# Gate logits as one stacked product, sample states in one burst, and small columns behind four tiles of x

## The chip, the cores and the metric

The kernel runs on one core of one Trainium2 chip. The core has a matrix engine (TensorE, PE in the profile, with PEld for its weight loads), a vector engine (VectorE, DVE), a scalar engine (ScalarE, ACT), GpSimd (POOL) and a queue engine (SyncE, SP), and 16 DMA engines. The metric is the device time of one execution in microseconds; a kernel is told by the median of its runs.

## What is computed

One step of a decoder with two post-norm layers over 1024 prompt tokens and 64 sample tokens (8 sequences of 8). Its first part is one projection x @ w_in, whose columns feed a gated linear attention (GLA), a forgetting attention, a short convolution and merge gates. The change touches only the GLA part:

```python
a_pre = jnp.einsum('btr,rk->btk', p['gla_a'], w_gla_a2) + b_gla_a          # r = 16
log_a = (jax.nn.log_sigmoid(a_pre.astype(jnp.float32)) / GLA_TAU).reshape(B, T, GLA_H, GLA_DK)
...
b = jnp.cumsum(log_a.astype(f32).reshape(B, N, C, H, DK), axis=2)
b_last = b[:, :, -1:]
...
k_end = kf * jnp.exp(b_last - b)
ds = jnp.einsum('bnthk,bnshv->bnhkv', k_end, vf)
def step(S, inp):
    d, dS = inp
    return d[..., None] * S + dS, S
```

The 16 columns `gla_a` times `w_gla_a2` are the gate logits. For the sample sequences one step gives the new state of each of 8 batches and 4 heads: the old state decayed, plus ds.

## The kernel before, in words

The work stands in four stages; the change lies in the first, `stage_front`. Every engine has its own program, written out in order, and engines wait for each other on semaphores that only count up. Nothing is scheduled automatically: an engine's order is the order of the code in its block.

**Projection.** x is loaded in 9 tiles of up to 128 tokens (`load_x` on SP), transposed by TensorE (`transpose_x`, 8 transposes a tile into a ring of 6 banks) and split into a high part `xh` (ScalarE, `x_heads`) and a low part `xl` (VectorE, `x_tails`). Weights come in blocks of 128 columns (`load_block`, two raw buffers) and are split likewise: ScalarE's `head(n)` writes `w_hi`, VectorE's `tail(n)` writes `w_lo` and so frees the raw buffer, for which the load of block n + 2 waits. A product is three matmuls, high by high, high by low, low by high, over 8 chunks of 128 rows.

**Units.** `FRONT` lists the order of the column blocks, and each entry makes units: three groups of tokens (384, 384, 320), or nine for v. `work` computes a unit into bank n % 2 and so waits until the unit two before it has been read out, which the reader tells by counting up `unit_free`. `place` reads a unit out, on ScalarE or VectorE by kind. The first entry, s, is a block of small columns: 8 of the forget logits and 16 of `gla_a` (at column 32), with zeros between. Its three units s0, s1, s2 stand among the transposes: s0 behind three tiles that have been split, s1 and s2 behind all nine. Then come the a units (gate logits, one FP32 matmul of `wa2` by `gaT` each), then the v units.

On ScalarE the head of block 1 and 2 stands behind the read-out of s0, that of block 3 behind s1's, and `place` of s copies `gaT` (line 594) and then the forget logits `z` (line 595), which gives the bank back.

On VectorE `place` of an s unit does nothing before the change. Its place in the order, for all three, is behind the splits of blocks 1, 2 and 3:

```python
            x_tails(0, 6)
            tail(0)
            x_tails(6, 18)
            tail(1)
            tail(2)
            tail(3)
            for n in range(first("s", 0), first("v", 0)):
                place(n)
```

**Recurrence.** For each pair of heads p, TensorE alternates `attend`, `new_state` and `outputs` per tile with `fill`, which computes quarters of projection units. After the last tile come the sample states: `new_sample_state` for two batches at a time, into banks 5 and 6, each of the later ones waiting for VectorE's `carry_sample` of the two before (`s0_new`), with a `fill` between. Scores are in banks 3 and 4. Then, for p = 0, the second a units.

## Time and profile before

| what | us |
|---|---|
| median of 3 runs | 1643.15 |
| the runs | 1642.85 to 1646.71 |
| the profiled execution | 1645.76 |
| its span, from first to last instruction | 1644.1 |
| TensorE busy in it | 1529.4 (93%) |
| VectorE busy | 829.7 (50%) |
| ScalarE busy | 663.8 (40%) |
| GpSimd busy | 236.1 (14%) |

The mean granted TensorE clock was 0.972 of 2.4 GHz. Times in the rows below count from the span's start. A busy time of TensorE includes matmuls that overlap, so the distance from one matmul's start to the next tells its price better than its length. Idle time of an engine off the critical path costs nothing.

### The profile page before, as it was taken

Reading aid. Unit: us, or ns where it says so; the run is one execution under the profiler, and the core shown is the slowest. Engines: PE = TensorE matmul, PEld = TensorE weight load, DVE = VectorE, ACT = ScalarE, POOL = GpSimd, SP = SyncE. Lnnn points to the kernel's source line nnn. Section 1 sums busy time; section 2 is a strip of 40 time slices with the busy share of each in tenths; the row PEclk is TensorE's granted clock in tenths of the full one; section 3 lists DMA queues with packets and bytes.
Section 4 is the critical chain, followed back from the end, with each engine's and each line's share of the span. In section 5 each row is a group of like instructions: output and inputs, shape, how many; then the busy total and the mean of one; then the engine's idle time right before and its main releaser. Section 6 shows DMA issues by size and latency. Waiting matters only on the chain. (4 is left out here: it accounts for less than half of the span.)

```text
span 1644.1 us, 26139 instructions
## 1 busy us (share of the span) xinstructions
PE 1529.4 (93%) x10051; PEld 1394.5 (85%) x10051; DVE 829.7 (50%) x1386; ACT 663.8 (40%) x1135; POOL 236.1 (14%) x295
## 2 busy tenths in 40 slices
PE   8999999999999998999999999999995799999980
PEld 7999899899987887889999999998784688888760
DVE  4422463353045654522332232223758699999975
ACT  5422242222255554422121121113111688888866
POOL 1000120013012111130000000000000334543310
PEclk9999999999999999999999999999996899999995
DMA  6121232134212121173261124103535799999646
GB/s 189 36 45 39 81 119 54 29 92 147 81 50 72 44 72 59 36 244 125 62 205 39 39 59 150 56 1 117 179 116 167 241 269 276 340 297 283 164 64 237
DMA packets 154229, 204.39 MB, mean 124 GB/s; under 512 B 14723, under 2 KB 121235, under 8 KB 154104
## 3 DMA queue, kind: packets, MB, share of 16 engines
q1 hardware_dynamic: 135224, 140.82, 27.4%
q0 software_dynamic: 18880, 61.89, 13.8%
q8 instruction: 80, 1.31, 0.3%
q14 instruction: 45, 0.37, 0.1%
HBM read 152.34 MB, written 50.34 MB: 123 GB/s over the span
## 5 line engine op out<-in xcount | busy, mean ns | idle before, releaser
L388 PE MATMUL ps<-xh,slab_hi 128*128 128x384 f32 (+1 forms) x504 | 170.4, 338 | 1.3 <-DVE slab_lo L752 1.3
L388 PE MATMUL ps<-xh,slab_lo 128*128 128x384 f32 (+1 forms) x504 | 165.0, 327 | 0.0
L388 PE MATMUL ps<-xl,slab_hi 128*128 128x384 f32 (+1 forms) x504 | 164.8, 327 | 0.0
L1921 PE MATMUL ps<-xh,slab_lo 128*128 128x384 f32 (+1 forms) x384 | 125.2, 326 | 0.0
L1921 PE MATMUL ps<-xh,slab_hi 128*128 128x384 f32 (+1 forms) x384 | 125.1, 326 | 0.0
L1921 PE MATMUL ps<-xl,slab_hi 128*128 128x384 f32 (+1 forms) x384 | 125.1, 326 | 0.0
L2137 DVE TENSOR_TENSOR gt_sg<-ps,gt_sg 128x384 f32<-128x384 f32 (+1 forms) x48 | 25.7, 536 | 187.6 <-PE ps L1921 187.5
L2913 PE MATMUL ps<-mo_hi_gu,mo_xh 128*128 128x512 f32 x256 | 100.3, 397 | 1.2 <-ACT mo_xh L3016 0.7
L388 PEld LDWEIGHTS ps<-xh,slab_hi 128*128 128x128 f32 x504 | 95.1, 189 | 6.7 <-issue 5.4
L2077 ACT ACTIVATE gt_sg<-ps 128x384 f32<-128x384 f32 (+1 forms) x48 | 22.7, 473 | 192.2 <-PE ps L1921 192.2
L2913 PE MATMUL ps<-mo_hi_gu,mo_xl 128*128 128x512 f32 x256 | 99.4, 393 | 0.0
L388 PEld LDWEIGHTS ps<-xl,slab_hi 128*128 128x128 f32 x504 | 95.1, 189 | 0.0
L388 PEld LDWEIGHTS ps<-xh,slab_lo 128*128 128x128 f32 x504 | 95.0, 189 | 0.0
L1921 PE MATMUL ps<-gt_oh,slab_hi 128*128 128x384 f32 (+1 forms) x288 | 94.0, 327 | 0.0
L1921 PE MATMUL ps<-gt_oh,slab_lo 128*128 128x384 f32 (+1 forms) x288 | 94.0, 326 | 0.0
L1921 PE MATMUL ps<-gt_ol,slab_hi 128*128 128x384 f32 (+1 forms) x288 | 94.0, 326 | 0.0
L2867 POOL DMA_INDIRECT acc_dram<-mo_y,mo_slot_idx x32 | 71.8, 2243 | 141.6 <-DMA acc_dram<-mo_y,mo_slot_idx 73.7
L3089 DVE TENSOR_TENSOR mo_lo_gu<-mo_raw_g,mo_hi_gu 128x2048 fp32r<-128x2048 f32 x32 | 73.3, 2290 | 15.4 <-issue 12.2
L2871 POOL MEMSET mo_small<- 128x1 f32 x1 | 0.1, 98 | 522.3 <-POOLq L74 522.3
L1218 PE MATMUL ps<-xh,slab_hi 128*128 128x384 f32 (+1 forms) x192 | 69.8, 363 | 5.7 <-ACT slab_raw L1340 3.9
L2920 PE MATMUL ps<-mo_lo_gu,mo_xh 128*128 128x512 f32 x256 | 67.2, 404 | 7.0 <-DVE mo_lo_gu L3089 6.9
L3089 DVE TENSOR_TENSOR mo_lo_gu<-mo_raw_u,mo_hi_gu 128x2048 fp32r<-128x2048 f32 x32 | 73.1, 2283 | 0.4 <-issue 0.3
(500 smaller groups left out, 4053.1 us busy)
## 6 DMA issues: line engine op xcount, KB each, us to landing
slab_raw<-in_w_in SPq DMA_DIRECT2D x60, 512.0 KB, 4.4
mo_raw_g<-in_w_e_gate SPq DMA_DIRECT2D x16, 1024.0 KB, 11.1
mo_raw_u<-in_w_e_up SPq DMA_DIRECT2D x16, 1024.0 KB, 14.6
mo_raw_d<-in_w_e_down SPq DMA_DIRECT2D x16, 1024.0 KB
gt_oh<-oT_hi SPq DMA_DIRECT2D x3, 2176.0 KB, 8.9
gt_ol<-oT_lo SPq DMA_DIRECT2D x3, 2176.0 KB, 13.8
slab_raw<-in_w_branch SPq DMA_DIRECT2D x24, 256.0 KB, 4.5
x_dram<-slab_raw SPq DMA_DIRECT2D x9, 512.0 KB, 5.2
```

The lines of the kernel that those rows point to most:

```text
L388: mm = eng.matmul(out, w[:, b, k, :], x[:, k, t0:t0 + tn], start=(k == 0 and j == 0), stop=(k == KC - 1 and j == 2), skip_group_check=True)
L1218: mm = eng.matmul(out, w[:, b % RH, k, :], x[:, k, t0:t0 + tn], start=(k == 0 and j == 0), stop=(k == KC - 1 and j == 2), skip_group_check ...
L1921: last = eng.matmul(out, w[:, s % 2, c, wk, :], x[:, k, t0:t0 + tn], start=(k == 0 and i == 0), stop=(k == ks[-1] and i == 2))
L2077: eng.activation(sg[:, v % 4, 0:tn], sh.ps[:, gate_bank(j, v), 0:tn], ACT.Sigmoid).then_inc(sg_ready, 1)
L2137: eng.tensor_tensor(sg[:, v % 4, 0:tn], sh.ps[:, branch_bank(v), 0:tn], sg[:, v % 4, 0:tn], ALU.mult).then_inc(mul_done, 1)
L2867: eng.indirect_dma_start(out=sh.acc_dram[:, :], out_offset=bass.IndirectOffsetOnAxis(ap=mo.slot_idx[:, i:i + 1], axis=0), in_=y[:, i % RY, ...
L2871: eng.memset(small[:, :], EPS / ALPHA ** 2).then_inc(small_set, 1)
L2913: eng.matmul(sh.ps[:, 2 + r, :], (xh, xl)[j][:, r, k, :], hi_gu[:, r, k].rearrange("p m n -> p (m n)"), start=(k == 0 and j == 0), stop=False)
L2920: last = eng.matmul(sh.ps[:, 2 + r, :], xh[:, r, k, :], lo_gu[:, r, k].rearrange("p m n -> p (m n)"), start=False, stop=(k == KC - 1))
L3089: eng.tensor_tensor(lo_gu[:, i % 2, :, m, :], from_raw(buf, side, KC), f32(hi_gu[:, i % 2, :, m, :]), ALU.subtract).then_inc(tail_gu, 1)
```

## The change

Three things are changed, all in `stage_front`.

The small columns: SP loads x tiles 0 to 3, not only 0 and 1, before the two loads of small columns. GpSimd then copies the 16 columns of `gla_a` to columns 64 and 96 of the raw block as well, so that s has three copies of them, and ScalarE's `head(0)` waits for those copies.

The gate logits: `wa2` is loaded three times, at rows 32, 64 and 96 of a cleared tile, and split into `wa2S` with high rows at 32 and 96 and low rows at 64. `gaS` holds the read-out of an s unit, 112 rows, high at 32 and 64 and low at 96. One matmul in F32R format then sums all three partial products. The low rows are subtracted on VectorE, in `place`, and it is VectorE's subtraction that now gives the unit's bank back. The a units wait until all three s units have been given back.

The sample states: `new_sample_states` computes those of all 8 batches at once, into banks 3 and 4, ahead of the four fills; it waits for the scores to be read. `carry_sample` on VectorE keeps its places.

```diff
+    GA_AT, GA_ROWS = (32, 64, 96), 112
...
-        gaT, wa2 = sb("gaT", [LR, TOK]), sb("wa2", [LR, 256])
+        gaS = sb("gaS", [GA_ROWS, TOK], F32R)
+        wa2, wa2S = sb("wa2", [GA_ROWS, 256]), sb("wa2S", [GA_ROWS, 256], F32R)
...
+        def new_bank(b):
+            return sh.ps[:, 3 + b // 4, 128 * (b % 4):128 * (b % 4) + DV]
...
+            eng.memset(wa2[:, :], 0.0)
             eng.memset(w_raw[:, 0], 0.0).then_inc(cleared, 1)
...
+            eng.wait_ge(w_in[0], 32)
+            for at in GA_AT[1:]:
+                last = eng.tensor_copy(w_raw[:, 0, :, at:at + LR], w_raw[:, 0, :, GA_AT[0]:GA_AT[0] + LR])
+            last.then_inc(cleared, 1)
...
-            load_x(0)
-            load_x(1)
+            for t in range(4):
+                load_x(t)
             eng.wait_ge(cleared, 1)
             for col, at, n in ((FF, 0, H_FOX), (GA, 32, LR)):
                 eng.dma_start(w_raw[:, 0, :, at:at + n], sh.w_in[0, :, col:col + n].rearrange("(k p) n -> p k n", p=128)
                               ).then_inc(w_in[0], 16)
-            for t in range(2, NT):
+            for t in range(4, NT):
                 load_x(t)
...
-            eng.dma_start(wa2[:, :], sh.w_gla_a2[0]).then_inc(c_in, 16)
+            for at in GA_AT:
+                eng.dma_start(wa2[at:at + LR, :], sh.w_gla_a2[0]).then_inc(c_in, 16)
...
                     if kind == "a":
-                        eng.wait_ge(s_out, 3)
+                        for m in range(3):
+                            freed(eng, "s", 0, m)
...
                 if kind == "a":
                     t0, tn = GROUPS[g]
-                    mm = eng.matmul(out, wa2[:, 128 * i:128 * i + 128], gaT[:, t0:t0 + tn], start=True, stop=True)
+                    mm = eng.matmul(out, wa2S[:, 128 * i:128 * i + 128], gaS[:, t0:t0 + tn], start=True, stop=True)
...
-                eng.wait_ge(c_in, 96)
+                eng.wait_ge(c_in, 128)
...
+                if i == NT:
+                    eng.wait_ge(s0_new, 4)
...
-            def new_sample_state(p, b2):
-                if b2 == 0:
-                    eng.wait_ge(kes_ready, p + 1)
-                    eng.wait_ge(s_ready, s_count(p, NCH))
-                else:
-                    eng.wait_ge(s0_new, 4 * p + b2)
-                for e in range(2):
+            def new_sample_states(p):
+                eng.wait_ge(kes_ready, p + 1)
+                eng.wait_ge(att_ready, NT * (p + 1))
+                for b in range(DB):
                     for h in range(2):
-                        mm = eng.matmul(sh.ps[half(h), 5 + e, 0:DV], kez_s[:, 2 * b2 + e, half(h)],
-                                        v[0:64, p, NT - 1, 128 * h:128 * h + 128], start=True, stop=True,
-                                        skip_group_check=True)
+                        mm = eng.matmul(new_bank(b)[half(h), :], kez_s[:, b, half(h)], v[0:64, p, NT - 1, 128 * h:128 * h + 128],
+                                        start=True, stop=True, skip_group_check=True)
                 mm.then_inc(dss_mm, 1)
...
+                new_sample_states(p)
                 for b2 in range(4):
-                    new_sample_state(p, b2)
                     fill(p, 3 * NT + b2)
...
-                eng.wait_ge(w_in[n % RW], 16 * (n // RW + 1) + (16 if n % RW == 0 else 0))
+                if n == 0:
+                    eng.wait_ge(cleared, 2)
+                else:
+                    eng.wait_ge(w_in[n % RW], 16 * (n // RW + 1) + (16 if n % RW == 0 else 0))
                 eng.activation(w_hi[:, place_of(n)], w_raw[:, n % RW], ACT.Copy).then_inc(w_head, 1)
...
                 if kind == "s":
                     if g == 0:
-                        eng.wait_ge(c_in, 96)
-                    eng.activation(gaT[:, t0:t0 + tn], bank[32:48, :], ACT.Copy).then_inc(s_out, 1)
-                    eng.activation(z[:, t0:t0 + tn], bank[0:8, :], ACT.Identity, bias=bf[:, :]).then_inc(free, 1)
+                        eng.wait_ge(c_in, 128)
+                        eng.activation(wa2S[:, :], wa2[:, :], ACT.Copy)
+                    eng.activation(z[:, t0:t0 + tn], bank[0:8, :], ACT.Identity, bias=bf[:, :])
+                    eng.activation(gaS[:, t0:t0 + tn], bank[0:GA_ROWS, :], ACT.Copy).then_inc(s_out, 1)
...
+                if kind == "s":
+                    eng.wait_ge(s_out, g + 1)
+                    if g == 0:
+                        low = slice(GA_AT[1], GA_AT[1] + LR)
+                        eng.tensor_tensor(wa2S[low, :], wa2[low, :], f32(wa2S[low, :]), ALU.subtract)
+                    low = slice(GA_AT[2], GA_AT[2] + LR)
+                    eng.tensor_tensor(gaS[low, t0:t0 + tn], bank[low, :], f32(gaS[low, t0:t0 + tn]), ALU.subtract).then_inc(free, 1)
...
-                        eng.wait_ge(dss_mm, 4)
+                        eng.wait_ge(dss_mm, 1)
...
-                eng.wait_ge(dss_mm, 4 * p + b2 + 1)
+                eng.wait_ge(dss_mm, p + 1)
...
-                    last = eng.scalar_tensor_tensor(out=S0[:, b, :], in0=S0[:, b, :], scalar=d, in1=sh.ps[:, 5 + e, 0:DV],
+                    last = eng.scalar_tensor_tensor(out=S0[:, b, :], in0=S0[:, b, :], scalar=d, in1=new_bank(b),
                                                     op0=ALU.mult, op1=ALU.add)
```

The program's order on VectorE at the start. `w_lo` is in `slab_lo`; the four rows of line 752 are `tail` of blocks 1 to 4. Before:

```order
L760 TENSOR_TENSOR xl<-ps,xh 128x4x128 [waits fr_x_head] x6
L752 TENSOR_TENSOR slab_lo<-slab_raw,slab_hi 128x1024 [waits fr_w_head]
L760 TENSOR_TENSOR xl<-ps,xh 128x4x128 [waits fr_x_head] x10
L760 TENSOR_TENSOR xl<-ps,xh 128x4x64 [waits fr_x_head] x2
L752 TENSOR_TENSOR slab_lo<-slab_raw,slab_hi 128x1024 [waits fr_w_head] x4
L976 COPY fr_cols<-ps 128x76 [waits fr_b2_mm]
```

After:

```order
L766 TENSOR_TENSOR slab_lo<-slab_raw,slab_hi 128x1024 [waits fr_w_head] x3
L787 TENSOR_TENSOR fr_wa2S<-fr_wa,fr_wa2S 16x256 [waits fr_s_out]
L789 TENSOR_TENSOR fr_gaS<-ps,fr_gaS 16x384
L789 TENSOR_TENSOR fr_gaS<-ps,fr_gaS 16x384 [waits fr_s_out]
L789 TENSOR_TENSOR fr_gaS<-ps,fr_gaS 16x320 [waits fr_s_out]
L766 TENSOR_TENSOR slab_lo<-slab_raw,slab_hi 128x1024 [waits fr_w_head]
L997 COPY fr_cols<-ps 128x76 [waits fr_b2_mm]
```

Four subtractions have come in, the one that gives back the bank of s0 behind the splits of blocks 1 to 3 and ahead of that of block 4.

ScalarE from the last x split to the first copy of an a unit (`fr_T`). Line 574, after it 587, is `head`: blocks 1 and 2, then 3, then 4. Before:

```order
L594 ACTIVATE fr_gaT<-ps 16x384 [waits fr_c_in,fr_unit_mm]
L595 ACTIVATE fr_wide<-ps,fr_bf 8x384
L574 ACTIVATE slab_hi<-slab_raw 128x1024 [waits fr_w_in1]
L574 ACTIVATE slab_hi<-slab_raw 128x1024 [waits fr_w_in0]
L594 ACTIVATE fr_gaT<-ps 16x384 [waits fr_unit_mm]
L595 ACTIVATE fr_wide<-ps,fr_bf 8x384
L574 ACTIVATE slab_hi<-slab_raw 128x1024 [waits fr_w_in1]
L594 ACTIVATE fr_gaT<-ps 16x320 [waits fr_unit_mm]
L595 ACTIVATE fr_wide<-ps,fr_bf 8x320
L574 ACTIVATE slab_hi<-slab_raw 128x1024 [waits fr_w_in0,fr_unit_mm]
L602 ACTIVATE fr_T<-ps,fr_bga 128x384 [waits fr_pool_s,fr_unit_mm]
```

After:

```order
L607 ACTIVATE fr_wa2S<-fr_wa 112x256 [waits fr_c_in,fr_unit_mm]
L608 ACTIVATE fr_wide<-ps,fr_bf 8x384
L609 ACTIVATE fr_gaS<-ps 112x384
L587 ACTIVATE slab_hi<-slab_raw 128x1024 [waits fr_w_in1]
L587 ACTIVATE slab_hi<-slab_raw 128x1024 [waits fr_w_in0]
L608 ACTIVATE fr_wide<-ps,fr_bf 8x384 [waits fr_unit_mm]
L609 ACTIVATE fr_gaS<-ps 112x384
L587 ACTIVATE slab_hi<-slab_raw 128x1024 [waits fr_w_in1]
L608 ACTIVATE fr_wide<-ps,fr_bf 8x320 [waits fr_unit_mm]
L609 ACTIVATE fr_gaS<-ps 112x320
L587 ACTIVATE slab_hi<-slab_raw 128x1024 [waits fr_w_in0,fr_unit_mm]
L616 ACTIVATE fr_T<-ps,fr_bga 128x384 [waits fr_pool_s,fr_unit_mm]
```

A copy of `wa2S` has come in, and the logits (`fr_wide`) now come ahead of the `gaS` copy that stands in for `gaT`.

On TensorE, at the end of the first pair of heads, the last sample matmuls of `outputs` (line 497, after it 511), the sample states (509, after it 520) and the first product of a unit behind them. Before:

```order
L497 MATMUL ps<-fr_T,fr_qz 64x128 [waits fr_o_mm,fr_state_in]
L497 MATMUL ps<-fr_T,fr_qz 64x128 x15
...
L509 MATMUL ps<-fr_wide 64x128 [waits fr_s_ready,fr_kes_ready]
L509 MATMUL ps<-fr_wide 64x128 x3
...
L388 MATMUL ps<-xh,slab_hi 128x384 [waits fr_w_tail,fr_unit_free0]
...
L509 MATMUL ps<-fr_wide 64x128 [waits fr_s0_new]
L509 MATMUL ps<-fr_wide 64x128 x3
```

After:

```order
L511 MATMUL ps<-fr_T,fr_qz 64x128 [waits fr_o_mm,fr_state_in]
L511 MATMUL ps<-fr_T,fr_qz 64x128 x15
...
L520 MATMUL ps<-fr_wide 64x128 [waits fr_att_ready,fr_kes_ready]
L520 MATMUL ps<-fr_wide 64x128 x15
...
L400 MATMUL ps<-xh,slab_hi 128x384 [waits fr_w_tail,fr_unit_free0]
```

The four groups of four matmuls (the second of them is shown as well; two more follow in the same way) have become one group of sixteen ahead of the fills. The profile counts two passes for each of these FP32 matmuls.

## Rows read from the trace of the kernel before

**Rows 1.** The page, the span in 40 equal slices: busy tenths of TensorE.

```profile
PE   8999999999999998999999999999995799999980
```

**Rows 2.** Busy time by stage: stretch, its length, PE, PEld, DVE, ACT, POOL, PEclk, DMA, GB/s.

```profile
0.00:40.00 40.00, 31.91 (x167) 28.39 (x168) 17.07 (x24) 21.11 (x34) 7.21 (x26) 0.92 0.68 194
...
800.00:1000.00 200.00, 200.00 (x1217) 200.00 (x1216) 59.32 (x78) 33.35 (x37) 0.00 (x0) 1.00 0.34 103
```

**Rows 3.** Timeline of TensorE in the front: start, length, instruction [idle before, releaser].

```profile
9.04 3.67 PE L408 MATMUL ps<-ident,fr_wide 128*128 128x128 f32 x16 [0.72 <-DMA fr_wide<-in_x_prompt]
13.99 0.66 PE L388 MATMUL ps<-xh,slab_hi 128*128 128x384 f32 x1 [1.28 <-DVE slab_lo L752]
...
19.57 4.30 PE L408 MATMUL ps<-ident,fr_wide 128*128 128x128 f32 x40
...
28.09 0.31 PE L388 MATMUL ps<-xh,slab_hi 128*128 128x320 f32 x1
...
31.46 0.31 PE L388 MATMUL ps<-xh,slab_lo 128*128 128x320 f32 x1
...
33.53 3.70 PE L377 MATMUL ps<-fr_gaT,fr_wa 16*128 16x384 f32 x6 [1.41 <-ACT fr_gaT L594]
37.15 0.58 PE L382 MATMUL ps<-slab_hi,xh 128*128 128x256 f32 x1
```

**Rows 4.** Timeline of ScalarE in the front.

```profile
11.54 1.05 ACT L574 ACTIVATE slab_hi<-slab_raw 128x1024 fp32r<-128x1024 f32 x1
...
31.87 1.06 ACT L574 ACTIVATE slab_hi<-slab_raw 128x1024 fp32r<-128x1024 f32 x1 [2.50 <-DMA slab_raw<-in_w_in]
32.95 0.43 ACT L594 ACTIVATE fr_gaT<-ps 16x320 f32<-16x320 f32 x1
33.41 0.52 ACT L595 ACTIVATE fr_wide<-ps,fr_bf 8x320 f32<-8x320 f32 x1
```

**Rows 5.** By stage as above, two half microseconds of the front: the last column is GB/s.

```profile
6.00:6.50 0.50, 0.50 (x4) 0.50 (x3) 0.07 (x1) 0.40 (x1) 0.50 (x1) 1.00 0.90 89
...
7.50:8.00 0.50, 0.50 (x4) 0.42 (x2) 0.47 (x1) 0.49 (x1) 0.42 (x2) 1.00 0.97 385
```

**Rows 6.** Timeline of GpSimd (first row) and of VectorE in the front.

```profile
3.55 0.29 POOL L270 CAST fr_mask<-fr_T 128x128 int32<-128x128 f32 x1
...
10.82 0.69 DVE L760 TENSOR_TENSOR xl<-ps,xh 128x512 fp32r<-128x512 f32 x1 [1.14 <-ACT xh L581]
...
26.87 2.36 DVE L752 TENSOR_TENSOR slab_lo<-slab_raw,slab_hi 128x1024 fp32r<-128x1024 f32 x2 [0.50 <-ACT slab_hi L574]
32.96 1.23 DVE L752 TENSOR_TENSOR slab_lo<-slab_raw,slab_hi 128x1024 fp32r<-128x1024 f32 x1 [3.73 <-ACT slab_hi L574]
```

**Rows 7.** By stage: the first v products, with the granted clock.

```profile
37.10:40.50 3.40, 3.40 (x16) 3.35 (x16) 0.00 (x0) 1.64 (x2) 0.00 (x0) 0.50 0.62 169
```

**Rows 8.** Timeline of TensorE around the first group of new sample states.

```profile
175.53 1.96 PE L497 MATMUL ps<-fr_T,fr_qz 64*64 64x128 f32 x32
177.42 0.41 PE L388 MATMUL ps<-xh,slab_hi 128*128 128x320 f32 x1
...
180.02 0.31 PE L388 MATMUL ps<-xh,slab_lo 128*128 128x320 f32 x1
180.26 0.65 PE L509 MATMUL ps<-fr_wide 64*64 64x128 f32 x8
180.84 0.41 PE L388 MATMUL ps<-xh,slab_hi 128*128 128x320 f32 x1
...
181.09 0.30 PE L388 MATMUL ps<-xl,slab_hi 128*128 128x320 f32 x1
```

**Rows 9.** Timeline at the second a units: TensorE, and ScalarE's copies of them.

```profile
196.16 1.56 PE L377 MATMUL ps<-fr_gaT,fr_wa 16*128 16x384 f32 x4
198.72 0.80 PE L377 MATMUL ps<-fr_gaT,fr_wa 16*128 16x320 f32 x2 [1.01 <-ACT fr_T L602]
...
198.11 1.03 ACT L602 ACTIVATE fr_T<-ps,fr_bga 128x384 f32<-128x384 f32 x2
```

More of the change, by code:

```diff
@@ L768, in place @@
                     eng.wait_ge(unit_mm, n + 1)
-                if kind == "k":
+                if kind == "s":
[5 more added lines that the diff above has]
+                    eng.tensor_tensor(gaS[low, t0:t0 + tn], bank[low, :], f32(gaS[low, t0:t0 + tn]), ALU.subtract).then_inc(free, 1)
+                elif kind == "k":
                     eng.wait_ge(e12, 2 * i + 2)
```

## The prediction

> **What bounds the kernel now.** I read the slices first: TensorE shows 8 or 9 tenths in nearly every slice up to about 1230 us [rows 1], and a long stage such as 800 to 1000 us is 200.00 us busy out of 200.00, while the first 40 us hold 31.91 us [rows 2]. The reader is to see that the front, which the change touches, lies at the head of one long queue of TensorE: whatever delays or advances TensorE there moves all that follows, unless a later wait hangs on something that did not move. So I price the change at two points of TensorE's timeline: the first v product at 37.15 us [rows 3] and the length of the pieces that are altered near 180 us, 196 us and 340 us.
>
> Then I followed TensorE through the front row by row [rows 3]: the transposes of the third x tile at 9.04 after a wait of 0.72 for its data, unit s0 from 13.99 after a wait for `w_lo` of the small columns, transposes again at 19.57, then s1, and s2 straight behind it at 28.09, ending at 31.46 + 0.31 = 31.77. The a products start at 33.53, after a wait of 1.41 for ScalarE's copy of `gaT`. That copy (32.95) stands in ScalarE's queue behind the split of weight block 3 (31.87), which waited 2.50 for its transfer [rows 4].
>
> **Small columns behind four tiles.** SP now issues x tiles 0 to 3 first. Gain: the third tile no longer waits behind the columns, so at most the 0.72 us goes, and the head of block 0 moves from 11.54 to 10.8 at best [rows 3, 4]. Price: the columns land later. In the trace the rate sinks to 89 GB/s while they move, and is back at 385 GB/s by 7.5 us, so they had landed by then [rows 5]. Two more tiles of 524 KB at 385 GB/s ahead of them cost 2.7 us: 10.2. GpSimd's two new copies of 128 x 128 elements are bounded by the 0.29 us of a cast of that size [rows 6]; they make 10.8. GpSimd has finished its clears by then or just after. So the columns arrive when the tiles do; I take -0.7 for s0, with bounds -0.72 and +1.8 (columns landing 2.5 us later than worked out). Two more small loads on SP and a clear of `wa2` on GpSimd lie ahead of nothing that is late: block 3, the transfer that is waited for, is issued only when block 1 has been split.
>
> **Stacked product: the wait it adds.** Unit s0's bank is now given back not by ScalarE but by VectorE, in `place("s", 0)`. In VectorE's queue that stands behind the splits of blocks 1, 2 and 3, as the order in the section on the change shows. Unit s2 writes the same bank, so s2 now waits for the split of block 3. Queued behind s2 on TensorE is everything else. Step by step: VectorE's split of block 1 ends at 26.87 + 1.18 = 28.05 (half of the 2.36 for two) [rows 6]; it comes 0.7 earlier by the step above, and 0.35 later for ScalarE's new copy of `wa2S` (256 columns; the 320-column copy takes 0.43 [rows 4]): 27.7. Head 3 started 31.87 - 28.05 = 3.8 later, its transfer in between: 31.5. The split on VectorE starts 1.09 behind it and takes 1.23 [rows 4, 6]: 32.6 to 33.8. Then VectorE's two new subtractions of 256 and 384 columns; a 512-column one took 0.69 [rows 6], so I take 0.35 + 0.52, between nothing and 1.4 for both: s2 starts at **34.7** where it started at 28.09. TensorE stands idle for some 7 us.
>
> How long s2 then takes is not in the trace, since it ran at the full level: 3.68. After the shorter idle at 32 us the granted clock was 0.50, the lower level of 1.2 GHz, with 16 v products of 256 columns in 3.40 us, or 0.2125 each [rows 7]. At that rate 24 products of 320 columns take 6.4 us. The nearest row is s0: 24 products of 384 columns took 5.58 (13.99 to 19.57), and at the rate of s2's 320 columns, 0.147 apiece, they would have taken 4.2; it began slow and recovered, at a price of 1.4 [rows 3]. I take the same 1.4: 5.1, bounds 3.68 and 6.4. s2 ends at **39.8**.
>
> **Stacked product: from s2 to v.** ScalarE's bias copy (0.52), then its stacked copy (0.43) [rows 4], then VectorE's subtraction of 320 columns (about 0.45): the first a product at 41.3. ScalarE puts the head of block 4 (1.06 as for block 3) behind its copy, so its first copy of an a product starts 2.0 after s2; at 0.51 each [rows 9] two of them end 3.1 after s2. The third a product waits for the first, the first v product for the second: 39.8 + 3.15 = **42.95**, against 37.15. The front loses **5.8 us**; with s2's bounds +4.4 to +7.1, and to +8.9 if the columns are late as well. The products themselves are cheaper: from 33.53 to 37.15 the old three took 3.62, the new three 1.65, and that is inside the sum. I leave the v products as slow at their beginning as before, since a stretch of the same kind stands ahead of them.
>
> The Trainium skill ("FP8 and Floating Point Precision", section TensorE Precision Notes) says that a true FP32 product makes four passes through the array. By that alone the three products would shrink to a quarter, 0.9 instead of 1.65 in the front, and likewise near 196 us; how far the trace bears that out is weighed among the rivals.
>
> At the second a unit (196.16) the first two products take 1.56 and the third waits 1.01 for ScalarE's copy at 198.11 [rows 9]. That copy waits for a splitting chain, not for the products, so it stays; of the gain only the third product is left, 0.80 against the 0.31 of a 320-column product: **-0.4**, bounds 0 and -1.0.
>
> **New sample states in one burst.** Before, four groups of eight passes; each interrupts the unit in progress. From the product at 180.02 to the one behind the group at 180.84 there are 0.82 us, and the next follows after 0.25 instead of 0.147: 0.82 - 0.147 + 0.10 = 0.78 a group, 3.1 for four. In a burst: the 32 passes at 175.53 took 1.89 up to 177.42 [rows 8]; with the turn into and out of the burst, 2.15. That gives -0.95 per pair of heads, **-1.9** for both, bounds -1.4 and -2.4. The waits on `s0_new` that go price nothing extra: a group that waits for it comes out of the same 0.78 that the first, which doesn't, costs. The new wait on `att_ready` has already been met by `outputs`, and `attend` of the second pair waits for updates that ended tens of microseconds ahead. VectorE's eight updates keep their places and have more slack.
>
> **Sum.** +5.8 - 1.9 - 0.4 = +3.5 us. Against the profiled execution's 1645.76 that is 1649.3; its span is 1644.1. The median of the three runs is 1643.15, 2.6 lower, and it is the median that I carry: **1646.7**.
>
> **Rivals.** (a) *The lower clock lasts longer.* Place: s2 and the first v products. If s2 runs wholly at 1.2 GHz it takes 6.4 (+1.3), and if the v products stay there another 3.4 us, as in the stretch of [rows 7], half of that is lost (+1.7): +6.5, 1649.7, slower. It decides from 1.4 us of extra loss on. For it: 7 us of idle where 1.4 sufficed for a fall. Against it: s0 recovered midway. 0.22.
> (b) *No second fall.* s2 brings the clock up and the short waits before v don't bring it down: the 1.7 that the v products lose now comes back: +1.8, 1645.0. Against it: just such waits led to the 0.50. 0.15.
> (c) *Columns late.* If they land 2.5 us after the estimate, s0 and all behind it go from -0.7 to +1.8: +6.0, 1649.2. For it: the rate of 89 GB/s. 0.08.
> (d) *The bank is free in time,* so that the change costs no wait: s0's gain, the burst and the a unit alone: -0.7 - 1.9 - 0.4 = -3.0, 1640.2. Against it: the order on VectorE. 0.05.
> (e) *The a products bound by the array,* not by ScalarE's copies: their 1088 columns at the 0.2125 per 256 of [rows 7] are 0.9 in place of the 1.65 from the first of them to v (-0.75), and in the second unit the third product's wait of 1.01 goes too: +3.5 - 0.75 - 1.0 = +1.75, 1644.9. Against it: the third product waited for ScalarE [rows 9]. 0.05. By the Trainium skill ("FP8 and Floating Point Precision", TensorE Precision Notes) this is how the time would come out; the row at 198.72 does not agree.
> The forecast itself, 0.42, and 0.03 for a gain beyond these.
>
> **How the numbers follow.** A measurement of this kernel can tell about 0.3%, 4.9 us, from no change. Faster than 1638.2 needs a gain that I have no row for: 0.03. Slower than 1648.1: (a), (c) and 0.05 of the forecast's own upper end: 0.35. The rest, 0.62, is within it. The range, 1642.3 to 1651.0, leaves out (d), the gain without a row and what (a) and (c) could add to each other; it takes in (b) and (e) with some of the burst's bounds below them, since the runs before alone lie up to 3.9 us apart.
>
> **What would show it.** Of the changed kernel: TensorE's first 320-column product of s2 near 34.7 with some 7 us of idle released by VectorE's subtraction into `gaS`; the first v product near 43; head 0 near 10.8; each burst near 2.1 us with no group inside the fills; the third a product near 196 us still waiting for ScalarE. I am wrong if s2 follows s1 at once, if the front's delay does not reach the end, or if the clock's levels in the front cost more than 1.5 us other than worked out.

## The result, and the profile after

The changed kernel is **slower by 0.3%**: 1649.8 us (median of 9 runs, 1646.88 to 1653.72) against 1644.4 (9 runs, 1642.85 to 1648.42) on the same chip, ratio 1.003 with an interval of 1.0021 to 1.0039. The forecast was 1646.7, within a range of 1642.3 to 1651.0. The profiled execution after took 1649.8 us with a span of 1648.2, 4.1 longer than before, at a mean granted clock of 0.966 (before 0.972). Of the runs further down, one of e10 (3856.59 us) and one of the kernel before (3717.15 us) took more than twice as long and are in no ratio.

TensorE in the front after, as [rows 3] show it before. Columns: start, length, instruction, [idle before, releaser].

```profile
4.72 5.08 PE L420 MATMUL ps<-ident,fr_wide 128*128 128x128 f32 x32 [4.72 <-DMA fr_wide<-in_x_prompt]
12.75 0.41 PE L400 MATMUL ps<-xh,slab_hi 128*128 128x384 f32 x1 [2.95 <-DVE slab_lo L766]
...
16.99 4.29 PE L420 MATMUL ps<-ident,fr_wide 128*128 128x128 f32 x40
...
32.81 0.61 PE L400 MATMUL ps<-xh,slab_hi 128*128 128x320 f32 x1 [7.17 <-DVE fr_gaS L789]
...
38.91 0.42 PE L429 MATMUL ps<-ident,fr_T 19*128 19x19 f32 x4
40.53 0.64 PE L389 MATMUL ps<-fr_gaS,fr_wa2S 112*128 112x384 f32 x2 [1.20 <-DVE fr_gaS L789]
41.62 0.64 PE L389 MATMUL ps<-fr_gaS,fr_wa2S 112*128 112x320 f32 x1 [0.44 <-ACT fr_T L616]
42.09 0.58 PE L394 MATMUL ps<-slab_hi,xh 128*128 128x256 f32 x1
```

The gap of 0.72 ahead of the third x tile is gone, s0 starts 1.24 earlier, and then TensorE stands still for 7.17 us ahead of s2 and waits for VectorE's write of `gaS`. The first v product comes at 42.09 instead of 37.15: **4.94 us lost in the front**.

VectorE behind that wait (compare [rows 6]):

```profile
24.21 2.36 DVE L766 TENSOR_TENSOR slab_lo<-slab_raw,slab_hi 128x1024 fp32r<-128x1024 f32 x2 [0.41 <-ACT slab_hi L587]
30.42 1.23 DVE L766 TENSOR_TENSOR slab_lo<-slab_raw,slab_hi 128x1024 fp32r<-128x1024 f32 x1 [3.85 <-ACT slab_hi L587]
31.67 0.42 DVE L787 TENSOR_TENSOR fr_wa2S<-fr_wa,fr_wa2S 16x256 fp32r<-16x256 f32 x1
32.10 1.04 DVE L789 TENSOR_TENSOR fr_gaS<-ps,fr_gaS 16x384 fp32r<-16x384 f32 x2
39.89 0.50 DVE L789 TENSOR_TENSOR fr_gaS<-ps,fr_gaS 16x320 fp32r<-16x320 f32 x1 [6.74 <-ACT fr_gaS L609]
```

and ScalarE, whose head of block 3 sets the second row above (compare [rows 4]):

```profile
10.29 1.06 ACT L587 ACTIVATE slab_hi<-slab_raw 128x1024 fp32r<-128x1024 f32 x1 [0.67 <-POOL slab_raw L290]
...
29.33 1.06 ACT L587 ACTIVATE slab_hi<-slab_raw 128x1024 fp32r<-128x1024 f32 x1 [2.70 <-DMA slab_raw<-in_w_in]
...
39.02 0.52 ACT L608 ACTIVATE fr_wide<-ps,fr_bf 8x320 f32<-8x320 f32 x1 [8.64 <-PE ps L400]
39.45 0.41 ACT L609 ACTIVATE fr_gaS<-ps 112x320 fp32r<-112x320 f32 x1
...
40.98 1.05 ACT L616 ACTIVATE fr_T<-ps,fr_bga 128x384 f32<-128x384 f32 x2 [0.18 <-PE ps L389]
```

The chain is read backwards: s2 waits for the subtraction at 32.10, that stands behind the split at 30.42, that waits for ScalarE's head at 29.33, and that for the transfer of block 3 (2.70).

Head 0, at 10.29, is released by GpSimd, whose copies of the columns stand straight behind its clears:

```profile
9.14 0.53 POOL L287 MEMSET slab_raw<- 128x512 f32 x1
9.73 0.53 POOL L290 COPY slab_raw<-slab_raw 128x128 f32<-128x128 f32 x2
```

So the columns had landed by 9.73, and it was GpSimd's queue, not a load, that head 0 and with it s0 waited for.

Stretches of the front and two later ones (compare [rows 2, 7]). Columns: stretch, its length, PE, PEld, DVE, ACT and POOL busy with instruction counts, granted clock, DMA share, GB/s.

```profile
0.00:40.00 40.00, 24.50 (x148) 23.38 (x148) 16.99 (x26) 17.05 (x31) 8.03 (x29) 0.87 0.64 182
12.75:16.95 4.20, 4.20 (x24) 4.20 (x25) 1.05 (x2) 0.00 (x0) 0.00 (x0) 1.00 1.11 302
27.90:32.80 4.90, 0.00 (x0) 0.02 (x1) 2.34 (x4) 1.06 (x1) 0.00 (x0) 0.50 0.58 154
32.80:38.90 6.10, 6.09 (x24) 5.92 (x24) 0.34 (x1) 0.00 (x0) 0.00 (x0) 0.56 0.30 84
...
42.10:45.00 2.90, 2.90 (x14) 2.90 (x14) 0.23 (x1) 1.64 (x2) 0.00 (x0) 0.50 0.61 168
202.00:205.40 3.40, 3.16 (x10) 3.02 (x11) 1.15 (x2) 3.13 (x11) 2.06 (x4) 0.50 0.63 151
800.00:1000.00 200.00, 200.00 (x1218) 200.00 (x1217) 60.93 (x81) 32.86 (x36) 0.00 (x0) 1.00 0.32 96
```

Three things are to be seen. s0 ran at the full 2.4 GHz from its first product: clock 1.00, and 24 products in 4.24 us. (So early the clock column alone does not tell it: in the trace of before it reads 1.00 from 13.99 to 16.80 too, where the products stand 0.32 us apart, twice the 0.17 of s0 after the change.) The clock was already at the lower level of 1.2 GHz while TensorE stood idle, so s2 ran at it almost to its end (0.56): 6.10 us. And the long stage from 800 to 1000 us is as dense as before, so it gives nothing back.

The burst and the second a units (compare [rows 8, 9]), both from TensorE's timeline:

```profile
184.63 0.31 PE L400 MATMUL ps<-xh,slab_lo 128*128 128x320 f32 x1
184.87 1.96 PE L520 MATMUL ps<-fr_wide 64*64 64x128 f32 x32
186.77 0.41 PE L400 MATMUL ps<-xh,slab_hi 128*128 128x320 f32 x1
...
199.58 0.33 PE L389 MATMUL ps<-fr_gaS,fr_wa2S 112*128 112x384 f32 x1
200.32 0.44 PE L389 MATMUL ps<-fr_gaS,fr_wa2S 112*128 112x384 f32 x1 [0.41 <-DVE fr_y L839]
202.24 0.64 PE L389 MATMUL ps<-fr_gaS,fr_wa2S 112*128 112x320 f32 x1 [1.47 <-ACT fr_T L616]
...
202.74 0.67 PE L400 MATMUL ps<-xh,slab_hi 128*128 128x384 f32 x1
```

From the product ahead of the burst to the one behind it there are 2.14 us. The third a product still waits for ScalarE, 1.47 where it was 1.01, and the clock falls at 202.0, just there; that it falls because of this wait is not shown (see e6 and e9 below).

Where the difference stands along TensorE's timeline (start of the same instruction, after minus before):

| at (us, before) | place | after - before |
|---|---|---|
| 37.15 | first v product | +4.94 |
| 175.53 | ahead of the first burst | +4.61 |
| 196.16 | second a units | +3.42 |
| 199.45 | behind them | +3.21 |
| 211.41 | transposes of the outputs | +4.51 |
| 332.27 | ahead of the second burst | +3.94 |
| 347.23 | behind it | +2.85 |
| 636.33 | end of the first layer's attention | +4.40 |
| 742.79 | behind the transposes of cached keys | +5.59 |
| 1589.61 | last expert stage | +2.59 |
| 1644.1 | end of the span | +4.1 |

Up to 347 us the difference is made where the change was made, but for the stretch from 199 to 332 us: there the fall of the clock at 202.0 takes 1.30 (+3.21 to +4.51), and 0.80 of it comes back as a shorter wait ahead of the transposes near 217 us (0.59 where it was 1.39). Behind 347 us the difference moves by 1 to 3 us either way without an altered instruction: a fall of the clock at 635.5, waits of 4.2 instead of 2.9 us in all for cached keys, and waits of 3.9 instead of 6.9 us for VectorE's splits in the experts' stage.

### The profile page after: what moved, and what is told of

Its sections match the earlier page's. It is cut to its first block and busy times, and to the rows that moved or that the text cites. A ratio compares the mean times of both kernels' runs of the same rounds, so it can differ in the third digit from the quotient of the medians.

```text
span 1648.2 us, 26143 instructions
## 1 busy us (share of the span) xinstructions
PE 1527.6 (93%) x10045; PEld 1397.7 (85%) x10045; DVE 831.7 (50%) x1390; ACT 664.0 (40%) x1136; POOL 233.4 (14%) x298
## 5 line engine op out<-in xcount | busy, mean ns | idle before, releaser
L2888 POOL DMA_INDIRECT acc_dram<-mo_y,mo_slot_idx x32 | 65.9, 2058 | 173.4 <-DMA acc_dram<-mo_y,mo_slot_idx 119.1
L1432 ACT ACTIVATE fx_PT<-ps 128x512 f32<-128x512 f32 (+3 forms) x96 | 43.7, 491 | 74.7 <-PE ps L1299 74.3
L3116 DVE TENSOR_TENSOR mo_lo_d<-mo_raw_d,mo_hi_d 128x2048 fp32r<-128x2048 f32 x31 | 71.0, 2290 | 5.2 <-ACT mo_hi_d L3021 4.6
```

Source lines behind the costliest of these rows:

```text
L1432: eng.activation(PT[:, h, 4 * c:4 * c + nt, :].rearrange("p t n -> p (t n)"), sh.ps[:, 5 + C % 2, 0:128 * nt], ACT.Copy).then_inc(pt_out, 1)
L2888: eng.indirect_dma_start(out=sh.acc_dram[:, :], out_offset=bass.IndirectOffsetOnAxis(ap=mo.slot_idx[:, i:i + 1], axis=0), in_=y[:, i % RY, ...
L3116: eng.tensor_tensor(lo_d[:, :, :], from_raw(raw_d, side, 2), f32(hi_d[:, :, :]), ALU.subtract).then_inc(tail_d, 1)
```

## The experiments

Theory: the loss is s2's wait for VectorE's give-back behind the split of block 3, and it is carried to the end. Rival: the wait is covered later, and the time is lost to something else, above all to the clock. All twelve kernels, each against the kernel before on its own chip; "s2 to v" is the time on TensorE from the transposes behind s2 to the first v product, "low" the mean time per run at 1.2 GHz, worked out from span and mean clock (two times the span times one minus the clock). The kernels e1 to e11 are described below the table:

| kernel | median, us | before | ratio, 95% interval | first v | s2 to v | low, us |
|---|---|---|---|---|---|---|
| the change | 1649.8 | 1644.4 | 1.0030 [1.0021, 1.0039] | 42.09 | 3.18 | 105.5 |
| e1 | 1645.14 | 1643.94 | 1.0003 [0.9991, 1.0014] | 34.98 | 5.84 | 103.1 |
| e2 | 1644.72 | 1643.94 | 1.0002 [0.9992, 1.0012] | 38.12 | 5.90 | 102.2 |
| e3 | 1644.40 | 1643.94 | 1.0005 [0.9994, 1.0015] | 36.67 | 5.65 | 99.4 |
| e4 | 1650.82 | 1643.94 | 1.0042 [1.0028, 1.0056] | 43.79 | 3.17 | 98.4 |
| e5 | 1640.46 | 1644.56 | 0.9971 [0.9959, 0.9983] | 34.39 | 3.17 | 97.4 |
| e6 | 1644.31 | 1644.56 | 0.9996 [0.9986, 1.0006] | 36.20 | 5.73 | 100.5 |
| e7 | 1644.09 | 1644.56 | 1.0001 [0.9989, 1.0012] | 32.27 | 3.17 | 103.0 |
| e8 | 1644.30 | 1644.56 | 0.9991 [0.9978, 1.0005] | 35.16 | 5.66 | 95.5 |
| e9 | 1640.55 | 1644.28 | 0.9981 [0.9972, 0.9991] | 32.27 | 3.17 | 95.4 |
| e10 | 1642.00 | 1644.28 | 0.9984 [0.9973, 0.9994] | 33.82 | 3.18 | 93.3 |
| e11 | 1642.08 | 1644.28 | 0.9987 [0.9975, 0.9999] | 34.98 | 3.17 | 92.2 |

The kernel before itself has its first v product at 37.15, 5.45 from s2 to v, and 96 to 98 us of low clock in its runs on the chips of e1 to e11.

**The stacked product alone (e4)**: the change with the old order of loads and the four groups of sample states.

```diff
-            for t in range(4):
-                load_x(t)
+            load_x(0)
+            load_x(1)
...
-                new_sample_states(p)
                 for b2 in range(4):
+                    new_sample_state(p, b2)
                     fill(p, 3 * NT + b2)
```

> The stacked product alone: the changed kernel with the old order of loads (two tiles, then small columns) and the old groups of sample states. Theory A (the parts add up): the first v product near 44.5 us, 7.4 later than before, less about 0.2 at the second a units but with a fall of the clock there; total 7 to 9 us above before, about 1652. Theory B (the loss came from the small columns or from the burst): within 3 us of before.

```profile
34.42 0.61 PE L400 MATMUL ps<-xh,slab_hi 128*128 128x320 f32 x1 [7.27 <-DVE fr_gaS L791]
```

The same wait, 7.27 us, the first v product at 43.79, and 6.9 us lost at the end, as the first theory had it or slightly less. The whole loss sits in this part.

**VectorE gives the bank back early (e1)**: the changed kernel, s0 read out ahead of the split of block 1, s1 ahead of that of block 3.

```diff
+            place(first("s", 0))
             tail(1)
             tail(2)
+            place(first("s", 0) + 1)
             tail(3)
-            for n in range(first("s", 0), first("v", 0)):
+            for n in range(first("s", 0) + 2, first("v", 0)):
                 place(n)
```

> The changed kernel with one thing moved: on VectorE the read-out of s0 and s1 stands ahead of the splits of blocks 1 and 3 (s0 before the split of block 1, s1 before that of block 3); s2's stays behind block 3. Theory A (the front's loss is the wait of s2 for a bank that VectorE gives back behind the split of block 3): s2 starts within 0.3 us of s1's end, near 26 us, the idle of 7.2 us is gone, the first v product stands near 34 us instead of 42.1, and the time falls by about 8 us against the changed kernel, to about 1641.5, some 3 us under the kernel before. Theory B (the loss is the added copies and subtractions and the F32R format themselves, the place in the queue is of no matter): the first v product stays beyond 40 us and the time within 2 us of 1649.8.

s2 follows s1 at once, the first v product comes 7.1 us earlier than after the change, and the time falls from 1649.8 to 1645.14 (from 1.0030 to 1.0003 of before). This is 5 us and not the 8 of the first theory, and only draws level with before. The 34.98 also hold s0's shorter length in this trace (4.27, where before had 5.58; more on this under e3). The next late thing, first on TensorE and then on VectorE:

```profile
33.18 0.98 PE L389 MATMUL ps<-fr_gaS,fr_wa2S 112*128 112x384 f32 x2 [3.62 <-DVE fr_gaS L789]
...
31.28 1.23 DVE L766 TENSOR_TENSOR slab_lo<-slab_raw,slab_hi 128x1024 fp32r<-128x1024 f32 x1 [3.46 <-ACT slab_hi L587]
32.54 0.50 DVE L789 TENSOR_TENSOR fr_gaS<-ps,fr_gaS 16x320 fp32r<-16x320 f32 x1
```

s2's own read-out stands behind the split of block 3 as well, so the a products now wait 3.62 for it: 5.84 from s2 to v, as much as with the old FP32 products.

**The parts alone.** The burst alone (e2), both pairs:

```diff
+                new_sample_states(p)
                 for b2 in range(4):
-                    new_sample_state(p, b2)
                     fill(p, 3 * NT + b2)
```

> The kernel before with the burst of new sample states alone. Theory A (each of the three dropped turns between fills and states costs TensorE some 0.3 us, nothing else moves): two bursts of about 2.1 us, and 1.9 to 2.4 us less in all, 1642.2. Theory B (VectorE's updates, which now all wait for one burst, or the banks of the scores hold something up): time within 0.7 us of before or above it, with a wait of TensorE for s0_new or att_ready that was not there.

```profile
195.88 1.56 PE L380 MATMUL ps<-fr_gaT,fr_wa 16*128 16x384 f32 x4
198.44 1.43 PE L380 MATMUL ps<-fr_gaT,fr_wa 16*128 16x320 f32 x2 [1.01 <-ACT fr_T L603]
...
198.40:205.20 6.80, 6.76 (x20) 5.90 (x21) 3.09 (x4) 3.52 (x11) 1.87 (x3) 0.50 0.73 202
```

In its place each burst gains 1.1 us (+0.82 ahead of the first and -0.28 at the a units, +3.62 and +2.53 around the second). The last line, a stretch as above, shows where the first one's gain goes: the clock falls behind the wait of 1.01, and the third a product takes 1.43 instead of 0.80. The wait alone is not the cause, since the kernel before, e3 and e8 have the same 1.01 there and no fall. No new wait for s0_new or att_ready came. At the end nothing shows: by the interval a gain of up to 1.3 us is possible, the 1.9 to 2.4 of the first theory is not.

The columns alone (e3):

```diff
-            load_x(0)
-            load_x(1)
+            for t in range(4):
+                load_x(t)
```

> The kernel before with x tiles 0 to 3 loaded ahead of the small columns, and nothing else. Theory A (transposes without the gap of 0.72 us let the granted clock rise some 9 us earlier, so that s0 runs at the full level): s0 starts near 12.6 us and its 24 products take 4.2 us instead of 5.6, the split of block 1, the load of block 3 and with them the first v product come 2.5 us earlier, near 34.6, total about 1642. Theory B (the early rise in the changed kernel's profile was chance): s0 ends only 0.7 to 1.2 us earlier and the total is within 1.2 us of before.

```profile
13.07 0.41 PE L388 MATMUL ps<-xh,slab_hi 128*128 128x384 f32 x1 [1.96 <-DVE slab_lo L752]
...
13.70:17.10 3.40, 3.40 (x12) 3.40 (x11) 0.42 (x1) 0.00 (x0) 0.00 (x0) 0.50 1.13 272
```

s0 starts 0.92 earlier, at the full level, and falls to 1.2 GHz after three products: it takes 5.83, and only 0.48 is left at v: the second theory held. Over all thirteen traces s0 takes either 4.24 to 4.27 or 5.58 to 5.83 us, with both orders of loads (4.24 in e6 and e8, whose front is that of before; 5.77 in e10 with the new order): the shorter one in three of six traces with the old order and in four of seven with the new. The 1.3 us that s0 seemed to gain after the change is that difference, not the change.

The burst for the second pair alone (e8), `new_sample_states(p)` for p = 1 and the four groups for p = 0:

> The kernel before with the burst for the second pair of heads alone; the first keeps its four groups. Theory A (what the burst loses again is lost behind the first pair, at the second a units): -1.1 us, 1642.9, with as much time at the low clock as before. Theory B (it is lost by chance falls anywhere): no difference between first and second pair, 1643.5 to 1644.5 and more time at the low clock than before.

```profile
333.88 1.96 PE L522 MATMUL ps<-fr_wide 64*64 64x128 f32 x32
335.77 0.44 PE L391 MATMUL ps<-xh,slab_hi 128*128 128x384 f32 x1
```

-2.59 ahead of it and -3.68 behind it, again 1.1. The median lies where the second theory had it, and the time at the low clock (95.5) is not above before, as the first had it. The time, 0.9991 with an interval across 1, neither shows nor excludes that the gain reaches the end.

**All read-outs ahead of the splits (e5)**: e1, and s1, s2 and the first a units read out on both engines ahead of the splits of blocks 3 and 4. The splits of block 4, which `place` of s2 had set off until then, are written out by themselves. The two lines that keep `place` of s from setting off a split are not shown.

```diff
...
-            head(3)
             place(first("s", 0) + 2)
             for g in range(3):
                 place(first("a", 0) + g)
+            head(3)
+            head(4)
...
+            place(first("s", 0))
             tail(1)
             tail(2)
-            tail(3)
-            for n in range(first("s", 0), first("v", 0)):
+            for n in range(first("s", 0) + 1, first("v", 0)):
                 place(n)
+            tail(3)
+            tail(4)
```

> The changed kernel with s0 read out ahead of the split of block 1 on VectorE, and s1, s2 and the a units read out on ScalarE and VectorE ahead of the splits of blocks 3 and 4. Theory A (the stacked product is slow only through its places in the queues): the first v product near 32.5 us, 1.5 to 2.5 earlier than with s0 and s1 alone moved (34.97), and about 1.5 us less in all, 1643.5. Theory B (a later split of blocks 3 and 4 delays the loads behind them): a wait for weights shows between 60 and 110 us and the total is 1645 or more.

```profile
32.84 0.65 PE L389 MATMUL ps<-fr_gaS,fr_wa2S 112*128 112x384 f32 x2 [1.20 <-DVE fr_gaS L790]
33.92 0.41 PE L389 MATMUL ps<-fr_gaS,fr_wa2S 112*128 112x320 f32 x1 [0.43 <-ACT fr_T L616]
34.39 0.54 PE L394 MATMUL ps<-slab_hi,xh 128*128 128x256 f32 x1
```

From s2 to v 3.17 us instead of 5.45, and the time is 0.9971 of before: **faster than both kernels**, by 3 us more than the first theory had. The first v product came later than its 32.5, with s0 at 5.82 in this trace. No product of the v units waits for the later splits.

**The stacked product mended, alone (e11), and with the columns (e10).** e11 is e4 with e5's order of read-outs, e10 the same with the new order of loads; e9 is e5 with the burst for the second pair only; this edit of e9 is shown.

```diff
-                new_sample_states(p)
+                if p == 1:
+                    new_sample_states(p)
                 for b2 in range(4):
+                    if p == 0:
+                        new_sample_state(p, b2)
                     fill(p, 3 * NT + b2)
```

> The kernel before with the stacked product alone (old order of loads, no burst) and its read-outs ahead of the splits. Theory A (the stacked product loses only through its place on VectorE): the wait of the third sum for its bank is gone, the first v product starts 1 to 2 us earlier than before (35.2 to 36.2), and the time is 1642 to 1643. Theory B (the gain of e5 comes from the columns' order): first v product at 37 or later, time 1644 or more.

> As e5, with no burst at all: the columns' order and the stacked product with its read-outs ahead of the splits. Theory A (the bursts bring nothing to the end, the front brings all): within 1 us of e5, 1640.5 to 1641.5. Theory B (both bursts' 1.1 us reach the end): 1642.7.

> The changed kernel with all its read-outs ahead of the splits (as in e5), but the first pair of sample states keeps its four groups; only the second pair's are written in one burst. Theory A: the first pair's burst gains 1.1 us in its own stage and pays about as much for the fall of the clock that follows it near the second a units, so this kernel equals e5 within 1 us (1640.5), and its profile has no fall between 195 and 218 us. Theory B: the first burst's gain is real and reaches the end: 1641.6 or more, and the fall between 195 and 218 us is there without the first burst too.

e11 came as the first theory had it: v at 34.98, 0.2 earlier still than its range, and 1642.08, so the gain is the stacked product's and does not need the columns' order. e10 adds nothing that shows (1642.00 on the same chip, between its two theories), though v comes 1.16 earlier in its profile. By the medians e9 is 1.45 below e10 on the same chip, but by the ratios only 0.0003, and the runs of the two overlap: that the second burst's 1.1 reaches the end is not shown. e9 is as fast as e5 by the medians (1640.55 and 1640.46), so the first burst brings nothing that shows. By the ratios e5 stands 0.001 lower, and the intervals overlap; a gain of 1 us from the first burst is not excluded.

The second a units of e9, on TensorE:

```profile
191.46 0.44 PE L389 MATMUL ps<-fr_gaS,fr_wa2S 112*128 112x384 f32 x1 [0.41 <-DVE fr_y L856]
193.37 0.42 PE L389 MATMUL ps<-fr_gaS,fr_wa2S 112*128 112x320 f32 x1 [1.47 <-ACT fr_T L632]
```

The same waits of 0.41 and 1.47 as after the change, and the product behind them takes 0.42, not 0.64: no fall. Of thirteen traces the six with the first pair's burst all have a fall that begins between 194 and 213 us, and of the seven without it none has. What in the burst leads to it is not shown. Nor does the fall take the whole gain each time: from 175 to 332 us, against before, the changed kernel, e1 and e5 come out 0.5 to 0.7 shorter, and e4, e9, e10 and e11, which have the stacked product without the first burst, 0.1 to 0.3 longer. In e2, e6 and e7 the same stretch is 2.0 to 4.1 longer, with a fall of 6.8 us or with two falls.

**The wait at the second a units (e6, e7)**: ScalarE reads out the first two a units ahead of the head copies that stood before them; e6 on e2, e7 on e5.

```diff
-                    serve(p, 3 * NT + b2)
-                if p == 0:
-                    for g in range(3):
-                        place(first("a", 1) + g)
+                    for n in finished(p, 3 * NT + b2):
+                        if units[n] == ("b", 0, 2):
+                            for g in range(2):
+                                place(first("a", 1) + g)
+                        place(n)
+                if p == 0:
+                    place(first("a", 1) + 2)
```

> The burst alone, and ScalarE reads out the first two of the second a units ahead of its head copy and block split (near 196 us). Theory A (the burst's 2.2 us are lost again to a fall of the clock in the thin stretch at the second a units, where TensorE waits 1.0 us for ScalarE): that wait shrinks below 0.3 us, the clock does not fall there, and the time comes to 1641 to 1642.5. Theory B (the burst's gain is lost elsewhere, such as a chain through ScalarE and the stores that fixes the transposes near 217 us): the stretch gets shorter but the total stays at 1643.5 to 1645, with a longer wait before the transposes of the outputs.

> The two above together with the whole change: stacked product with its read-outs ahead of the splits, small columns behind four tiles, burst, and the second a units read out first. Theory A (all gains are local and add up): about -4.5 at the first v product, -2.2 for the bursts, -1 at the second a units: 1637 to 1640, below both kernels. Theory B (what is gained in the front is given back in falls of the clock or at a later wait): 1642 to 1645.

Of e6, TensorE at the a units, ScalarE, and TensorE again:

```profile
194.44 2.38 PE L380 MATMUL ps<-fr_gaT,fr_wa 16*128 16x384 f32 x6
...
205.17 1.12 ACT L662 ACTIVATE fr_T<-fr_T 128x1088 f32<-128x1088 f32 x1 [1.86 <-DMA out_sample_gla<-fr_T]
...
217.37 0.63 PE L447 MATMUL ps<-ident,fr_wide 128*128 128x128 f32 x4 [2.30 <-DVE fr_wide L961]
```

and two stretches of e6 as above:

```profile
197.60:201.00 3.40, 3.40 (x12) 3.40 (x11) 1.62 (x3) 3.26 (x11) 2.47 (x4) 0.50 0.53 141
218.10:221.50 3.40, 3.40 (x13) 3.40 (x12) 1.18 (x2) 2.16 (x3) 1.12 (x2) 0.50 0.89 287
```

The wait is gone, and the place behind the a units is 2.70 ahead of before. The clock falls all the same, at 197.6, with no wait of TensorE ahead of it but 0.02: the first theory of e6 had the wait as the cause, and this it is not, or not alone. Then ScalarE waits 1.86 (before 0.96) for the store of the sample rows, and the transposes of the outputs wait 2.30 (before 1.39) for what follows from it: at 217 us only 0.21 of the 2.70 is left. A second fall, at 218.1, takes 1.5 more: at 264 us the kernel is 1.33 behind. The second theories of e6 and e7 hold. e7 is 7.09 ahead at 199 us and 0.24 behind at 332, with a wait of 3.60 ahead of the same transposes and falls at 212.4 and 267.0. A wait on the path had hidden a store behind it.

## Why the prediction came out as it did

**Direction and mechanism** held: the bank's give-back behind the split of block 3, idle time of some 7 us (7.17), released by VectorE's write of `gaS`; the rival by which the bank would be free in time fell.

**The small columns**: s0 was put 0.7 earlier; it came 1.24 earlier, and head 0 at 10.29 instead of 10.8. The columns had landed when GpSimd was done with its clears (9.73), so the rival of late columns fell too; that GpSimd's copies and not the tiles would set head 0 had been priced (10.8) but not as the step that s0 waits for. At the end none of it shows (e3; e10 against e11): the gain is smaller than what s0's two lengths give and take.

**s2's start**: 34.7 worked out, 32.81 measured. The step that failed is where everything ahead was taken from the one trace of before: s0 took 4.24 instead of 5.58 this time, and the split of block 1 ended at 25.39 where 27.7 was worked out. From there to s2 it took 7.4 against 7.0.

**s2's length**: this term was mis-sized. I took s0's loss of 1.4 over (5.1); it took 6.10 at the lower level, close to the upper bound of 6.4. That is the first half of rival (a). Its second half, v products slow for another 3.4 us, did not come: the level rose near the end of s2 and fell again at 41.6, for one stretch of 3.4. So the front is +4.94 against +5.8, from two errors that offset each other: 1.9 too late and 1.0 too short. That rival (a)'s time, 1649.7, is so near the 1649.8 is chance: the larger part of what it adds did not come.

**From s2 to v**: 3.15 worked out, 3.18 measured, in every kernel whose read-outs do not wait for block 3. The figure held, one step behind it did not: ScalarE's first copy of an a product was not late by the head of block 4, it waited 0.18 for the product itself (40.98), and e5, where that head comes later, has the same 3.17. I counted this gain inside the sum and did not see that it is most of the change's worth: 2.3 to 2.7 us, had the read-outs stood ahead of the splits. The sum of rival (d), a bank that is free in time, leaves it out: with it, by the same rows, -5.2 instead of -3.0, and e5, where the bank is free in time, measured -4.1.

**Rival (e)**, products bound by the array: by the Trainium skill ("FP8 and Floating Point Precision", TensorE Precision Notes) a true FP32 product makes four passes. The traces agree: at 1.2 GHz the second FP32 product of [rows 3], 384 columns, took 1.28 us (34.53 to 35.81 in the trace of before), and by the v products of [rows 7] at that level, 0.2125 for 256 columns, a product that passes once takes 0.32. What the rival had wrong is what sets the pace once the products are cheap: in the changed kernel it is ScalarE's copies and the waits, 1.56 us from the first stacked product to v where the rival had 0.9, and at the second a units 2.66 from the first to the third, where it had been 2.56. The second a units gain 0.21, not 0.4, because the clock falls at their third product: in e4, e9, e10 and e11, where it doesn't, they take 2.91 against 3.30, the 0.4 as worked out.

**The bursts**: 0.95 each worked out, 1.1 measured in place. The step that failed is that a gain in its stage was carried on whole. Of the first burst's 0.95 and the a units' 0.4 the changed kernel keeps 0.67 at 332 us, since a fall of the clock follows in all six traces that have this burst.

**The sum**: +3.5 forecast; +5.4 by the medians (+3.5 to +6.4 by the interval), +4.0 by the two profiled executions. Of the 3.1 us between 1646.7 and 1649.8, 1.25 is the level that I started from, since nine runs of before have a median of 1644.4 where three had 1643.15. The other 1.9 is what the change costs beyond +3.5: up to 385 us the traces show +2.8, and what follows behind it is not settled by one trace each. The runs after spend some 9 us more at 1.2 GHz than those of before on other chips (105.5 against 96 to 98); on a busy stretch half of that is lost. That is where the rest can have gone, but the runs don't show it piece by piece.

## What to carry to other kernels

When a step's read-out moves to another engine, look at what stands ahead of it in that engine's queue, down to the transfer that it waits for: the same stacked product cost 6.9 us (e4) or gained 2.2 (e11, by the interval 0.2 to 4.1) by its read-outs' place behind or ahead of two splits. Mend the whole chain at once, since with the first wait gone (e1) the second took its place, and with the a units' wait gone (e6) a store did. A gain of 1 us in a stage counts only when runs show it at the end, and where one trace differs from the next by 1.4 us in an untouched unit, compare stretches that don't contain it, such as s2 to v, rather than starts.

## What the runs showed of the hardware

- After the change the clock fell to 1.2 GHz at 27.9, 2.3 us into the idle stretch ahead of s2, and stayed there for 10.2 us, though products ran without a gap from 32.81 on. In e4, the other kernel with such a stretch, it stayed for 10.2 as well. The other falls in the fronts and near 200 us lasted 3.4 or 6.8 us.
- With the same idle times (0.41 and 1.47 us) ahead of the same products the clock fell in the changed kernel, e1 and e5, which have the first pair's burst, and not in e4, e9, e10 and e11, which don't. In e6 it fell at the same place with 0.02 us of idle time.
- s0, 24 products of 384 columns, takes about 4.25 or about 5.7 us, in seven and six of thirteen traces, whatever the order of loads. In e3 its first three products ran at the full level, behind an idle time of 1.96, and the next eleven at half of it, without idle time in between.
- The waits for cached keys near 700 us add up to 2.9 us in the trace of before and 4.2 in that of after, with no edit there.
